# Summing the squares of the gated SSD output: TensorE accumulates four tiles instead of GpSimd adding them first

## The reference

```python
gated = (y.reshape(bt, L, D_INNER) * jax.nn.silu(z.astype(f32))).reshape(bt, L, SSM_GROUPS, D_INNER // SSM_GROUPS)
y = rmsnorm(gated, norm_g.reshape(SSM_GROUPS, D_INNER // SSM_GROUPS)).reshape(bt, L, D_INNER)
return y.astype(h.dtype) @ w_out, new_conv, new_state.astype(ssm_state.dtype)

def rmsnorm(x, g):
    y = xf * lax.rsqrt(jnp.mean(xf * xf, axis=-1, keepdims=True) + EPS)
```

## Time and profile before

| | us |
|---|---|
| median of 3 runs | 2051.27 (2045.62 to 2056.36) |
| the profiled execution | 2056.36 |
| its span in the trace | 2054.7 |
| PE busy | 1904.2 (93% of the span) |
| DVE busy | 1182.1 (58%) |
| ACT busy | 960.6 (47%) |
| POOL busy | 509.0 (25%) |
| mean granted TensorE clock | 0.965 of full speed |

### The profile page before, as it was taken

The page is one execution under the profiler, slowest core; times in us unless marked ns, Lnnn a source line. Parts: engine busy times, 40 slices in busy tenths (PEclk is TensorE's granted clock), DMA queues, the critical chain, the costliest instruction groups (busy, mean ns, idle before and its releaser), DMA issues. The chain is left out here.

```text
span 2054.7 us, 37590 instructions
## 1 busy us (share of the span) xinstructions
PE 1904.2 (93%) x14678; PEld 1804.1 (88%) x14678; DVE 1182.1 (58%) x2048; ACT 960.6 (47%) x1571; POOL 509.0 (25%) x535
## 2 busy tenths in 40 slices
PE   6899987999999879999997878999998999699999
PEld 4899987999999669999895658999988999699998
DVE  4668774555444446554446765555475778555544
ACT  3666663444343334443443554443356666444432
POOL 3122221343100304431103302342111222124420
PEclk9899998999999899999999999999998999899999
DMA  6357764555574536555657725655563776456554
GB/s 175 111 189 236 235 200 131 164 164 155 156 210 147 185 103 176 164 155 155 190 186 260 278 72 152 167 164 147 163 187 115 229 227 218 119 163 170 164 147 136
DMA packets 501554, 352.64 MB, mean 172 GB/s; under 512 B 14730, under 2 KB 486204, under 8 KB 500604
## 3 DMA queue, kind: packets, MB, share of 16 engines
q1 hardware_dynamic: 493508, 304.52, 51.0%
q0 software_dynamic: 7440, 45.43, 5.9%
q10 hardware_dynamic: 430, 0.29, 0.1%
HBM read 326.58 MB, written 50.63 MB: 184 GB/s over the span
## 5 line engine op out<-in xcount | busy, mean ns | idle before, releaser
L268 PE MATMUL ps<-xh,whi 128*128 128x288 f32 x2368 | 656.8, 303 | 10.1 <-PEq L176 9.9
L268 PE MATMUL ps<-xl,whi 128*128 128x288 f32 x2368 | 646.4, 299 | 0.0
L240 DVE TENSOR_TENSOR wlo<-raw,whi 128x2048 fp32r<-128x2048 f32 (+3 forms) x241 | 501.8, 2083 | 247.3 <-ACT whi L229 247.2
L229 ACT ACTIVATE whi<-raw 128x2048 fp32r<-128x2048 f32 (+3 forms) x241 | 419.2, 1741 | 263.6 <-PE ps L276 216.2
L268 PEld LDWEIGHTS ps<-xh,whi 128*128 128x128 f32 x2368 | 453.8, 192 | 12.3 <-issue 10.6
L268 PEld LDWEIGHTS ps<-xl,whi 128*128 128x128 f32 x2368 | 454.6, 192 | 0.7
L276 PE MATMUL ps<-xh,wlo 128*128 128x288 f32 x2368 | 353.3, 300 | 0.0
L276 PEld LDWEIGHTS ps<-xh,wlo 128*128 128x128 f32 x2368 | 327.2, 189 | 1.1
L520 POOL TENSOR_TENSOR gh<-sg,ut 128x288 f32<-128x288 f32 x88 | 216.3, 2458 | 352.5 <-ACT sg L461 352.5
L268 PE MATMUL ps<-hh,whi 128*128 128x288 f32 x704 | 189.7, 296 | 0.0
L268 PE MATMUL ps<-hl,whi 128*128 128x288 f32 x704 | 189.6, 297 | 0.0
(11 more groups left out here) (323 smaller groups left out, 2682.3 us busy)
## 6 DMA issues: line engine op xcount, KB each, us to landing
raw<-in_ffn_w_in SPq DMA_DIRECT2D x176, 512.0 KB, 5.0
raw<-in_ssm_w_in SPq DMA_DIRECT2D x80, 512.0 KB, 4.9
raw<-in_ffn_w_out SPq DMA_DIRECT2D x64, 384.0 KB, 4.1
raw<-in_ffn_w_out SPq DMA_DIRECT2D x64, 320.0 KB, 3.3
H<-in_state_ssm SPq DMA_DIRECT2D x32, 512.0 KB, 7.6
out_ssm_sample<-H SPq DMA_DIRECT2D x32, 512.0 KB, 6.5
raw<-in_ssm_w_out SPq DMA_DIRECT2D x32, 512.0 KB, 5.2
Kp_L<-in_cache_diff_k SPq DMA_DIRECT2D x64, 256.0 KB, 4.7
```

The lines of the kernel that those rows point to most:

```text
L229: act.activation(wts["hi"][:, s, 0:width], raw[:, s, 0:width], ACT.Copy).then_inc(hi_ready.sem, 1)
L240: dve.tensor_tensor(wts["lo"][:, s, 0:width], raw[:, s, 0:width], wts["hi"][:, s, 0:width].bitcast(F32), ALU.subtract).then_inc(lo_ready.s ...
L268: pe.matmul(out, W[0][:, kk, j, :], x_[:, k, :], stop=False, start=(part == 0 and kk == 0 and x_ is seg.hi), skip_group_check=True)
```

## The change

POOL's 24 additions go away (12 for each SSD layer), and with them the signal `sq_added`. PE takes the four squared tiles itself: `sum_squares(g, chunks)` issues one matmul by ones for each chunk, all into the same 288 columns of bank 6, the first with `start`, the last with `stop`, and waits for ACT's `squared` before each. After the loop, group 3 is cut in two: chunks 12 and 13 before `turn_tail` 2 to 5, chunks 14 and 15 behind them.

```diff
-                def sum_squares(g):
-                    pe.wait_ge(sq_added.sem, sq_added.at(3 * g + 3))
-                    pe.matmul(ps[:, 6, 0:TOK], ones, sq[:, 0, :], start=True, stop=True,
-                              skip_group_check=True).then_inc(sq_summed.sem, sq_summed.inc())
+                def sum_squares(g, chunks):
+                    for c in chunks:
+                        pe.wait_ge(squared.sem, squared.at(c + 1))
+                        mm = pe.matmul(ps[:, 6, 0:TOK], ones, sq[:, c % 4, :], start=(c == 4 * g),
+                                       stop=(c == 4 * g + 3), skip_group_check=True)
+                    if c == 4 * g + 3:
+                        mm.then_inc(sq_summed.sem, sq_summed.inc())
...
-                        sum_squares(g)
+                        sum_squares(g, range(4 * g, 4 * g + 4))
...
+                sum_squares(GROUPS - 1, (CI - 4, CI - 3))
                 for q in range(2, 6):
                     turn_tail(q)
-                sum_squares(GROUPS - 1)
+                sum_squares(GROUPS - 1, (CI - 2, CI - 1))
...
-                def add_square(c):
-                    pool.wait_ge(squared.sem, squared.at(c + 1))
-                    if c % 4 > 1:
-                        pool.wait_ge(sq_added.sem, sq_added.at(c // 4 * 3 + c % 4 - 1))
-                    pool.tensor_tensor(sq[:, 0, :], sq[:, 0, :], sq[:, c % 4, :], ALU.add).then_inc(
-                        sq_added.sem, sq_added.inc())
...
-                    if k % 2 == 0 and k >= 4:
-                        for c in (k - 4, k - 3):
-                            if c % 4:
-                                add_square(c)
...
-                for c in range(CI - 3, CI):
-                    add_square(c)
```

More of the change, by code:

```diff
@@ L800, in ssd @@
              fs_mm, fs_moved, outer, updated, ys_mm, y_mm, yoff_mm, off_scaled, y_taken, off_added, z_scaled, z_ready,
-             gated, squared, sq_added, sq_summed, y_logged, y_rstd, normed, tl_mm, tl_moved) = (
+             gated, squared, sq_summed, y_logged, y_rstd, normed, tl_mm, tl_moved) = (
                  S(n) for n in (
@@ L805, in ssd @@
                      "y_state_product", "y_product", "y_off_product", "off_scaled", "y_taken", "off_added", "z_scaled",
-                     "z_ready", "gated", "gated_squared", "gated_squares_added", "squares_in", "y_logged", "y_rstd", "y_normed", "tail_turned",
+                     "z_ready", "gated", "gated_squared", "squares_in", "y_logged", "y_rstd", "y_normed", "tail_turned",
                      "tail_moved"))
```

## The result

| | before | after | ratio after / before |
|---|---|---|---|
| median, timed together | 2053.67 us (6 runs) | 2064.45 us (6 runs, 2061.40 to 2068.09) | 1.0058 [1.0037, 1.0080] |
| the same again | 2055.01 us | 2066.53 us (`after_again`) | 1.0049 [1.0032, 1.0066] |

The change makes the kernel 0.5 to 0.6% slower: +10 to +12 us by the ratios. I had forecast +6.8 us. The measured 2064.45 us lies above the forecast's own range (2051.7 to 2060.0) and inside the wide one (2048 to 2066).

The account below looks back on a forecast made before the run. PE was taken to bound the loop, with only the phase end latency-bound. Terms 5.9 + 1.3 - 0.4 gave +6.8 us, 2058.1 us on the median of 2051.27; own range 2051.7 to 2060.0, wide range 2048 to 2066.

Parts of the forecast that it names:

- Term 1: Loop sums of groups 0 and 1, both layers: three more PE matmuls each, fully paid, +5.9 us (bounds 0 and 5.9).
- Term 2: Group 2's sum before iteration 15: partly covered by ACT's weight split, 0.66 us a layer, +1.3 us in all.
- Term 3: Group 3 behind the loop: POOL's adds go, two matmuls delay the tails; +0.2 layer 0, -0.6 layer 3, together -0.4 us.
- The gate: DVE's gate of chunk 15, layer 3, behind the loop: 0.95 us beside POOL's add, to be back at 0.46 us.
- the blocking rule: At that gate: DVE with two SBUF inputs and GpSimd reading SBUF contend, second blocked; predicted end 1773.45, trace 1773.31.
- Everything is paid: Rival: group 2 costs all 1.48 us per layer, pair ahead of tails delays ACT fully; +10.4 us, 2061.7 us; chance 0.17.
- The loop hides the matmuls: Rival: ACT or the DMAs set the iterations, only the end changes; -0.4 us, 2050.9 us; chance 0.07.
- DVE freed from POOL: Rival: without POOL's 24 adds DVE gives time back everywhere; -12.5 us with the +6.8, 2038.8 us; chance 0.04.

Follow-up runs that it names:

- after_again: The changed kernel timed once more, unchanged, beside the same runs of before: 2066.53 us, ratio 1.0049.
- e1: Against before: PE sums groups 0 to 2 by four matmuls each, group 3 keeps POOL's adds; 2063.94 us, ratio 1.0049.
- e8: Against before: three more unused fp32 matmuls ahead of each loop sum, POOL's adds all kept; 2065.57 us, ratio 1.0055.
- e7: Against after: squares and ones in fp32r, one record a matmul instead of two; 2053.89 us, 0.9992 of before.
- e4: Against before: twelve more fp32 matmuls ahead of each loop sum, results overwritten, POOL's adds untouched; 2086.55 us, ratio 1.0159.
- before_again: The kernel before, unchanged, timed against itself: 2056.14 us, ratio 1.0002.
- e5: Against after: POOL's adds put back as dead work into a scratch tile nobody reads; 2061.52 us, 1.0033 of before.
- e2: Against before: only group 3 summed as in after, two matmuls ahead of the tails, two behind; 2058.06 us, ratio 1.0014.
- e3: Against after: all four matmuls of group 3 behind the tails; 2060.36 us, 1.0029 of before.
- e6: Against before: group 2's matmul moved into iteration 15; in group 3 POOL adds only chunk 13, three matmuls behind the tails; 2051.82 us, ratio 0.9980.
- before_third: A third profile of the kernel before, nothing changed; one execution, 2049.03 us.
- after_third: A third profile of the changed kernel, nothing changed; one execution, 2066.03 us.

## Why the prediction was right, and where it was not

**Right in direction and in mechanism, on the border in size.** Slower, and by PE's matmuls in the loop: e1 has the loss, e8 makes it with three unused matmuls, e7 takes it away with cheap ones. I had given 0.76 to less than 0.5% and 0.20 to more; the two timings say 0.58% and 0.49%, both intervals hold 0.5%, so they don't decide it. That 2064.45 us fell inside 2048 to 2066 is partly luck: it is 4.5 us above what the terms allowed at most (2.4 of them because before's own median came out at 2053.67 and not 2051.27), and the second timing's 2066.53 is just outside.

**Term 1, groups 0 and 1: forecast +5.9, measured +5.8 us** (four times 1.45). The bound of zero is out: e4 pays 0.485 us for every matmul.

**Term 2, group 2: forecast +1.3, measured about +0.6 us.** ACT's weight split covers part, as said: `spread` is 0.55 us later in layer 0 (forecast 0.66), the wait for the root 2.96 us (forecast near 3.0). What I took as nothing was partly there: from `spread` to `y_across` it is 4.55 us (291.02 to 295.57), against 4.88 before (293.06 to 297.94), as the mean granted clock of that stretch was 0.62 and not 0.57. Over three profiles of each, iteration 15 is 0.3 us longer in the mean of either layer. That is less than it varies by itself (12.1 to 12.9 us in before, 12.4 to 13.4 in after), so the size of this term is known only roughly.

**Term 3, behind the loop: forecast -0.4, measured -0.9 and -1.1 us, -2.0 in all.** This is the term of the sum that was mis-sized where the change itself is. In layer 0, from `y_across` to the root, it is 8.23 us (302.24 to 310.47) where I had 9.6, and before had 9.39 (304.35 to 313.74). Two steps failed. I ran the last pair at half clock, 2.32 us to the root; it ran at full clock, 1.27 (309.20 to 310.47). And the first tail was ready 0.3 us sooner, as PE got its full clock just as the tails began. Windows on PE after, layer 0: the pair ahead of the tails, then the last pair.

```profile
302.83:304.75 1.92, 1.92 (x6) 0.50 1.13 339
309.20:310.44 1.24, 1.24 (x4) 1.00 0.19 56
```

The layer 3 forecast of -0.6 against a measured 8.63 - 7.97 = -0.7 is right by two errors that cancel: the pair ahead of the tails ran largely at half clock (1.74 us to the first tail, not 0.99; ACT waited 6.10, not 4.5), and the last pair at full. I had taken the clock of each place in before's trace for the clock in after's. Moving work moves it.

**The gate.** In layer 3 the gate of chunk 15 went from 0.95 to 0.46 us, with no add of POOL beside it. The doubled gate is no fixed cost of the kernel before, though: its third profile has no add beside a gate and none that is longer. The doubling comes again in before_again and, in layer 0, in e4: 0.95 us for the gate at 325.28, begun 0.16 us behind an add of 0.79 that ends at 325.91. The Trainium skill, "SBUF — State Buffer", section "Who interferes with whom", has the blocking rule that I set beside the row. By it that gate would end at 325.91 + 0.45 = 326.36 us; the trace of e4 has 326.23, so it agrees within 0.13. In e5, where POOL's add starts after the gate is done, it is 0.46 us as well:

```profile
1772.99 0.46 DVE L1652 TENSOR_TENSOR G<-yt,Zs 128x288 f32<-128x288 f32 x1
...
1775.36 1.51 POOL L1215 TENSOR_TENSOR sqx<-sq 128x288 f32<-128x288 f32 x2 [12.21 <-ACT sq L1383]
```

**The sum, and what it left out.** With the measured terms it is about +4.4 us, less than my +6.8. The time says +10 to +12. So the forecast is nearer than its working deserves: terms 2 and 3 too high by 2.4 us together, and about 6 to 7.5 us that no term held. They are not at the change. The profiles show where such time can lie (the middle, +3.9 us in the means) and by what (the granted clock in one stretch, a DMA's landing in another), but single profiles of one program differ as much.

**The rivals.** "Everything is paid", +10.4 us, has the number but not the mechanism: group 2 did not cost 1.48 us a layer, and the end gained. "The loop hides the matmuls" fell with the 14.18 us iterations and with e4. "DVE freed from POOL" fell too: the loop without POOL's adds (e1) is no faster anywhere, and DVE's busy time fell by 1.3 us in all. POOL's own fell by 14.1 us, not by the 19.3 that I had multiplied out.

**What stays open.** Seven kernels with small shifts of PE's work come out 2 to 7.5 us above their own price: after and e2 clearly, e1 and e3 at the edge of their intervals, e5, e7 and e8 within them. Two do not: e6, and e4 with its 33 us. The missing adds are an unlikely cause: e2 keeps 18 of the 24 and is 5.4 us above, e8 keeps all and is 4.0 above. A fixed delay for whatever makes PE later isn't it either: e2's loop is that of before, and e6's profile starts its middle, like the others, at another time.

A part goes with the granted clock. Every execution is on record with its mean granted clock. Over the 82 of before that were timed beside the experiments, 0.001 less clock goes with 1.6 us more (a fitted line; the executions scatter by 2.5 us about it). An estimate from that line, mean against mean on one chip: e2 ran at 0.9654 where before ran at 0.9675, which is worth all of its 3.1 us; e8's lower clock (0.9650 against 0.9680) is worth 4.6 of its 11.3, after_again's (0.9663 against 0.9675) 1.8 of 9.7. But e3 ran at the higher clock (0.9680 against 0.9669) and is all the same 1.9 us above its price, 3.6 at equal clock. So the clock is a part of the excess and not all of it.

What would fit is that the moment at which PE arrives in the later layers decides how often it meets half clock or a late transfer there. But with three profiles of before and after, in which the stretches outside the change together vary by 5 and 7 us, I can't show it, and no run here sets that moment alone.

## What to carry over

An engine that is busy for all of an iteration, as PE is here, pays every added instruction at its full streaming length, so price it from a row where such instructions follow each other, and multiply; work that an idle engine does for it is worth keeping, however clumsy. Where PE waits anyway, the same matmul is free, so put the moved sum there and not ahead of what another engine is waiting for. And when a forecast is a few us in 2000, a sum over the stretches that change is only half of it: time the kernel against itself, and be ready for as much again from stretches that nobody touched.

## What the runs showed of the hardware that I had not expected

- The same unchanged stretch costs 40.0 to 44.1 us, and in one program, after, 41.0 or 44.1. At 1200 to 1240 us of before, between the same two instructions, it is 40.0 us in before, before_again, e4, e5 and e8, 41.0 to 42.3 in before_third, after and e3, 40.9 in e7, and 44.0 to 44.1 in after_again, after_third, e1, e2 and e6. The granted clock makes the difference, as the windows above show for 2.7 of the 4.1 us.
- A second stretch, 1005 to 1015 us, takes 10.1 to 10.4 us in the three profiles of before and 12.6 to 12.9 in after and e1. There ACT waits for weights. Timeline on ACT in before and then in e1:

```profile
1010.64 1.92 ACT L229 ACTIVATE whi<-raw 128x2048 fp32r<-128x2048 f32 x1 [2.57 <-DMA raw<-in_diff_w_qkv]
```

```profile
1014.16 1.91 ACT L229 ACTIVATE whi<-raw 128x2048 fp32r<-128x2048 f32 x1 [3.92 <-DMA raw<-in_diff_w_qkv]
```

  In e2 the same wait was 5.55 us.
- A third stretch lies at 1556.9 us of before, ahead of layer 3's loop, and goes the other way. From the first product of `products_cb` (L990) to `sums_of_chunk` it is 9.61 us at half clock in before, before_again, after_third, e1, e2, e4, e6, e7 and e8, and 5.5 us at full clock in before_third, after, after_again, e3 and e5. Windows on PE in before, then in before_third:

```profile
1556.94:1566.55 9.61, 9.61 (x41) 0.50 0.01 2
```

```profile
1555.22:1560.72 5.50, 5.50 (x40) 1.00 0.01 3
```

  In the eleven profiles of after and the experiments the middle runs from 1254.8 to 1268.5 us. These 4.1 us hide the losses of the other two stretches in the first profile of after, whose middle looks like that of before (1257.8 against 1257.5 us). They are also most of why PE was busy only 5.5 us longer there, though 24 matmuls of 0.483 us are 11.6. The three middles of before agree within 0.3 us partly by the same chance: before_third loses 1.4 us at 1200 to 1240 us and gets 4.1 back here.
- An iteration of 13.53 us is 15.05 to 15.08 in ten of the fourteen profiles, of before and of changed kernels, and oftenest at one of two places: from iteration 5 to 6 of layer 0 (five profiles) and from 9 to 10 of layer 3 (six). The start of the program up to the first `y_across` takes 110.4 to 116.5 us, and that whole range comes in the three profiles of before.
- fp32r against fp32 for this sum: 0.78 us for four records against 2.11 for eight, to the end of the last matmul. In the loop that was 0.05 us more an iteration instead of 1.45.
